# Three expert routers of a one-core transformer kernel without their unread TensorE products

## The chip, the cores and the metric

The kernel runs on one NeuronCore of a Trainium2 chip. The metric is the device time of one execution in microseconds. Five engines work side by side and meet at semaphores: TensorE (PE: matmuls; PEld: its weight loads), VectorE (DVE), ScalarE (ACT), GpSimd (POOL) and SyncE (SP), which issues the weight transfers.

## The reference

A sequence of 256 tokens of width 1024 goes through three layers, all in float32. Each has a mixer and a mixture of experts:

```python
x = x + token_mixer(rms_norm(x), ...)              # first block
x = x + hierarchical_moe(rms_norm(x), ...)         # 32 experts, hidden width 256   ("one")
x = layer_norm(ALPHA * x + even_mixer(x), ...)     # second block, layer 0
x = layer_norm(ALPHA * x + hierarchical_moe_2(x))  # 32 experts, hidden width 512   ("l0")
x = layer_norm(ALPHA * x + fourier_mixer(x), ...)  # second block, layer 1
x = layer_norm(ALPHA * x + hierarchical_moe_2(x))  # 32 experts, hidden width 512   ("l1")
```

A router takes, for each token, the best of four groups of eight experts, then the two best experts of that group, and weighs them by a softmax. An expert computes `(silu(x @ w_gate) * (x @ w_up)) @ w_down` on the tokens that chose it. The weights of all experts are read: 101 MB for stage one (32 x 3 x 1 MB) and 201 MB each for l0 and l1 (32 x 3 x 2 MB).

## The kernel before, in words

For each of the three expert layers, tagged one, l0 and l1, the kernel runs `stage_out_route` and then `stage_experts`, which calls `stage_packed`.

`stage_out_route` is the end of the mixer and the router, on two halves of 128 tokens (j = 0, 1). TensorE multiplies the mixer's result by the output weights (`out`, L1713, four groups), turns the normalised rows with transposes (`turn`, L1721) and computes 36 logits a token (`logits`, L1729). VectorE adds the residual and normalises a half (L1828 in one, L1831 and L1832 in l0 and l1) before TensorE may turn it; ScalarE copies the turned rows into `hT` (L1767) before the logits may read them. When both halves' logits are there, VectorE reads them (L1862 with a bias, L1864 without) and selects groups and experts in a chain of small operations, ending at `sel` (L1877). TensorE then counts, with ten small matmuls (L1750), how many tokens an expert has and the place of each; VectorE reads the places at L1898 (l0, l1) or L1908 (one).

`keep_busy(k, bank, n)` (L199) issues n matmuls of the identity with itself, 128 x 512, into a PSUM bank that nobody reads; each is two matmul instructions in the profile (L203). In the router they stand at three places of TensorE's queue: after the first half's logits, after the second half's logits, and after the counts. There are 4, 3 and 2 in stage one, 4, 3 and 1 in l0, and 4, 2 and 1 in l1. TensorE takes its queue in order and does not wait for anything before one of them.

`stage_packed` gathers the tokens of a pass by multiplication with one-hot tiles, which VectorE makes first (L2299). The first gather (L2147, L2148) is 32 matmuls of 128 columns, ScalarE copies it into `hT` (L2263), and a pass follows: gate product, up product, down product (L2154), with SiLU on ScalarE (L2271). Stage one has eleven passes of three experts, the other two have sixteen passes of two. In stage one alone a single `keep_busy` stands ahead of the first gather (L2207).

Weights come in chunks through a ring in on-chip memory: seven chunks of 3 MB in stage one, eleven of 2 MB in l0 and l1. SyncE issues the transfer of a chunk (L2034 in one, L2036 in l0 and l1) when `s_used` says that the chunk whose place it takes has been multiplied. Before the router has ended the ring is filled ahead; the next transfer then waits for the first chunk that the gate product of pass 0 releases. The same queue also carries the next stage's small tables and weights.

Of the kernel before, what the change touches and what calls it, by code (L numbers as in the profile page):

```python
# [192 lines left out]
def bc(ap, axis, n):  # L193

    shape = list(ap.shape)
    return ap.unsqueeze(axis).broadcast_to(shape[:axis] + [n] + shape[axis:])


def keep_busy(k, bank, n):  # L199

    ident = k.table("ident")
    for _ in range(n):
        k.nc.tensor.matmul(bank, ident, bc(ident, 1, W // P), start=True, stop=True)  # L203
# [1382 lines left out]
class FinalTail:  # L1586

    tag = "final"
# [64 lines left out]
def stage_out_route(k, tag, alpha, rr, ex, ahead, rows_first=None):  # L1653
# [15 lines left out]
    with scope:  # L1669
# [21 lines left out]
        tp = k.ps(f"turned_ps_{tag}", [P, 2, W])  # L1691
# [8 lines left out]
        with nc.Block() as block:  # L1700
            @block.sync
            def _(sp):
                ahead(sp, s_y)
                if bias is None:
                    sp.wait_ge(s_t, 4)
                    sp.wait_ge(s_low, NJ)
                    ex.load(sp, 1)

            @block.tensor
            def _(pe):  # L1710
                def out(j, n):
                    for c in range(KC):
                        last = nc.tensor.matmul(y[:, j, n, :], k.hT[:, c, j * P:(j + 1) * P],  # L1713
                                                w_out[:, c, n * W:(n + 1) * W], start=(c == 0), stop=(c == KC - 1))
                    last.then_inc(s_y, 1)

                def turn(j):
                    pe.wait_ge(s_h, j + 1)
                    for n in range(2):
                        for c in range(4):  # L1720
                            last = nc.tensor.transpose(turned[2 * j + n][:, c * P:(c + 1) * P],  # L1721
                                                       rows[:, j, 4 * n + c:D:KC], k.table("ident"))
                        last.then_inc(s_t, 1)

                def logits(j):
                    for c in range(KC):
                        if c % 4 == 0:
                            pe.wait_ge(s_ht, 2 * j + c // 4 + 1)
                        last = nc.tensor.matmul(lp[:, j, :], k.hT[:, c, j * P:(j + 1) * P], w[:, c, :],  # L1729
                                                start=(c == 0), stop=(c == KC - 1))  # L1730
                    last.then_inc(s_p, 1)

                pe.wait_ge(k.s_out_w, k.out_loads)
                out(0, 0)
                out(0, 1)
                out(1, 0)
                turn(0)
                out(1, 1)
                pe.wait_ge(s_wl, 16)
                logits(0)  # L1740
                keep_busy(k, tp[:, 0], 4)
                turn(1)
                logits(1)
                keep_busy(k, tp[:, 0], 2 if tag == "l1" else 3)
                pe.wait_ge(s_sel, 1)
                pe.wait_ge(s_rl, 16 if w_bias is None else 32)
                for j in (NJ, *range(NJ)):
                    for i in range(min(j + 1, NJ)):
                        t = before if i == j else ones
                        last = nc.tensor.matmul(counts if j == NJ else pp[:, j], t, sel[:, i], start=(i == 0),  # L1750
                                                stop=(i == min(j, NJ - 1)))
                    if j >= NJ - 1:
                        last.then_inc(s_pos, 1)
                keep_busy(k, tp[:, 0], 2 if ex.ways == 3 else 1)

            @block.scalar
            def _(act):
# [762 lines left out]
class EvenTail:  # L2520

    tag = "f"
# [477 lines left out]
class FourierTail:  # L3000

    tag = "fourier"
# [333 lines left out]
```

## Time and profile before

| what | value |
|---|---|
| median of 3 runs | 1812.33 us (1811.42 to 1812.88) |
| the profiled execution's own time | 1813.08 us |
| its span, first to last instruction | 1809.5 us |
| mean granted TensorE clock | 0.981 |
| TensorE busy | 93% of the span |
| VectorE, ScalarE, GpSimd busy | 37%, 22%, 3% |
| read from memory | 578.62 MB |

A timeline row has the start in microseconds from the span's start, the duration, the engine, the line of the kernel, the operation, what it writes and reads, its shape, and in brackets how long the engine had been idle before it and what it waited for. Rows of one line that follow each other are merged, with their count (x8). Durations of matmuls include their latency, so that pipelined ones overlap: the pitch is read from starts. The granted clock (PEclk) is a share of 2.4 GHz: 1.00 is 2.4 GHz, 0.50 is 1.2 GHz.

### The profile page before, as it was taken

The page shows a single profiled execution, that of the slowest core. Times are in us where ns is not written, and L with a number is a line of the kernel's source. Part 1 is how long each engine was busy: PE and PEld are TensorE (multiplying, and loading weights), DVE is VectorE, ACT ScalarE, POOL GpSimd, SP SyncE. Part 2 cuts the span into 40 slices and gives each one's busy share as a digit, 9 for nine tenths or more (in the row PEclk, how much of TensorE's full clock was granted, in tenths as well). Part 3 has the DMA queues.
Part 4 walks back from the last instruction along what each step waited for, and adds up shares of the span by engine and source line. Part 5 has one row for each costly group of instructions (what it writes and reads, how often), then busy time and mean ns, then how long its engine had stood idle before and what let it go on. Part 6 is the DMA issues. An engine that isn't in the chain of part 4 may idle for free. (4 is left out here: it accounts for less than half of the span.)

```text
span 1809.5 us, 21999 instructions
## 1 busy us (share of the span) xinstructions
PE 1678.2 (93%) x9162; PEld 875.4 (48%) x9162; DVE 661.0 (37%) x1392; ACT 389.8 (22%) x690; POOL 62.6 (3%) x67
## 2 busy tenths in 40 slices
PE   7999999999998779999999999889979999999895
PEld 6785445684654445555344444334543444434442
DVE  3468576563442235443222212122441122222123
ACT  2411333342222122312111111011211111111111
POOL 0000000600000003100000000000000000000000
PEclk9999999999999999999999999999989999999998
DMA  5343432109899978448999999999958999999995
GB/s 216 137 132 140 160 119 51 48 23 427 339 429 428 429 329 311 158 179 359 423 428 428 427 427 428 427 428 419 420 231 370 428 427 427 428 428 426 427 424 207
DMA packets 66949, 583.28 MB, mean 322 GB/s; under 512 B 19420, under 2 KB 21596, under 8 KB 31774
## 3 DMA queue, kind: packets, MB, share of 16 engines
q1 hardware_dynamic: 62093, 580.21, 77.6%
q10 hardware_dynamic: 4752, 1.61, 0.5%
q8 instruction: 75, 1.23, 0.3%
q14 instruction: 29, 0.23, 0.0%
HBM read 578.62 MB, written 3.15 MB: 321 GB/s over the span
## 5 line engine op out<-in xcount | busy, mean ns | idle before, releaser
L2154 PE MATMUL up_ps_l<-room,hT 128*64 128x512 f32 x800 | 214.3, 600 | 10.9 <-DMA room<-in_expert_w_up 9.4
L2154 PE MATMUL gate_ps_l<-room,hT 128*64 128x512 f32 x704 | 197.2, 601 | 13.3 <-DMA room<-in_expert_w_gate 7.8
L2154 PE MATMUL y_ps_l<-room,hidden_l 128*64 128x512 f32 x736 | 202.0, 595 | 4.3 <-ACT hidden_l L2278 2.3
L415 PE MATMUL proj_ps<-room,hT 128*128 128x512 f32 x288 | 124.6, 592 | 0.0
L2154 PEld LDWEIGHTS up_ps_l<-room,hT 128*64 128x64 f32 x800 | 67.9, 138 | 114.3 <-issue 113.5
L2154 PEld LDWEIGHTS gate_ps_l<-room,hT 128*64 128x64 f32 x704 | 63.9, 138 | 117.7 <-issue 117.7
L2377 DVE SCALAR_TENSOR_TENSOR y_low_l<-y_ps_l,slot_gate_l,y_high_l 128x512 fp32r<-128x512 f32 x64 | 47.9, 751 | 193.8 <-ACT y_high_l L2288 193.8
L2154 PE MATMUL gate_ps_l<-late_room,hT 128*64 128x512 f32 x320 | 113.6, 616 | 1.5 <-DMA late_room<-in_expert_w_gate 1.4
L2154 PEld LDWEIGHTS y_ps_l<-room,hidden_l 128*64 128x64 f32 x736 | 63.6, 137 | 105.4 <-issue 95.0
L407 PE MATMUL proj_ps<-hT,room 128*128 128x256 f32 x512 | 113.6, 384 | 0.0
L407 PEld LDWEIGHTS proj_ps<-hT,room 128*128 128x128 f32 x512 | 98.1, 192 | 15.3 <-issue 1.8
L2154 PE MATMUL y_ps_l<-late_room,hidden_l 128*64 128x512 f32 x288 | 102.8, 596 | 1.5 <-ACT hidden_l L2278 1.2
L2367 DVE TENSOR_TENSOR hidden_l<-hidden_l,up_ps_l 128x512 f32<-128x512 f32 x32 | 22.0, 687 | 214.6 <-PE up_ps_l L2154 214.6
L2288 ACT ACTIVATE y_high_l<-y_ps_l,slot_gate_l 128x512 fp32r<-128x512 f32 x64 | 44.0, 687 | 205.7 <-PE y_ps_l L2154 205.3
L2154 PE MATMUL up_ps_l<-late_room,hT 128*64 128x512 f32 x224 | 84.9, 595 | 2.8 <-DMA room<-in_expert_w_up 1.4
L415 PEld LDWEIGHTS proj_ps<-room,hT 128*128 128x128 f32 x288 | 54.7, 190 | 66.7 <-issue 66.5
L2271 ACT ACTIVATE hidden_l<-gate_ps_l 128x512 f32<-128x512 f32 x32 | 34.7, 1086 | 217.6 <-PE turn_ps_l L2221 217.6
L2314 DVE SCALAR_TENSOR_TENSOR x<-x,gather_ps_l 128x512 f32<-128x512 f32 x64 | 42.5, 684 | 97.7 <-PE gather_ps_l L2182 97.6
L2147 PE MATMUL gather_ps_l<-onehot_l,h_high_l 128*128 128x256 f32 (+1 forms) x288 | 73.5, 293 | 2.0 <-DVE onehot_l L2299 2.0
L2263 ACT ACTIVATE hT<-gather_ps_l 128x512 f32<-128x512 f32 x64 | 38.2, 597 | 169.0 <-PE gather_ps_l L2148 169.0
L2148 PE MATMUL gather_ps_l<-onehot_l,h_low_l 128*128 128x256 f32 (+1 forms) x288 | 72.1, 288 | 0.0
L2147 PEld LDWEIGHTS gather_ps_l<-onehot_l,h_high_l 128*128 128x128 f32 x288 | 57.1, 198 | 6.1 <-DVE onehot_l L2299 3.9
(636 smaller groups left out, 2347.5 us busy)
## 6 DMA issues: line engine op xcount, KB each, us to landing
room<-in_expert_w_up SPq DMA_DIRECT2D x50, 2048.0 KB, 28.2
room<-in_expert_w_down SPq DMA_DIRECT2D x46, 2048.0 KB, 33.2
room<-in_expert_w_gate SPq DMA_DIRECT2D x44, 2048.0 KB, 31.2
room<-in_moe_by_pass SPq DMA_DIRECT2D x22, 3072.0 KB, 30.5
late_room<-in_expert_w_gate SPq DMA_DIRECT2D x20, 2048.0 KB, 28.8
late_room<-in_expert_w_down SPq DMA_DIRECT2D x18, 2048.0 KB, 24.4
room<-in_w_in_blocks SPq DMA_DIRECT2D x17, 2048.0 KB, 8.0
late_room<-in_expert_w_up SPq DMA_DIRECT2D x14, 2048.0 KB, 32.0
```

The lines of the kernel that those rows point to most:

```text
L407: last = mm(pp[:, n % 2, m * T:(m + 1) * T], wbuf[n % 2][:, c, m * P:(m + 1) * P], k.hT[:, c, :], start=(c == 0), stop=(c == KC - 1))
L415: last = mm(pp[:, n % 2, j * W:(j + 1) * W], k.hT[:, c, j * P:(j + 1) * P], wbuf[n % 2][:, c, :], start=(c == 0), stop=(c == KC - 1))
L2147: mm(at, k.h_high[:, j, c], moving, start=(j == 0), stop=False)
L2148: last = mm(at, k.h_low[:, j, c], moving, start=False, stop=(j == NJ - 1))
L2154: return mm(of[q * TW:(q + 1) * TW], lhsT, rhs, **flags)
L2263: nc.scalar.activation(xg(n * per[b], per[b])[:, :, 0:width], got, ACT.Copy).then_inc(s_xg, 1)
L2271: nc.scalar.activation(hid[:].rearrange("p (c n) -> p n c", c=HT), G[:, 0:H].rearrange("p (n c) -> p n c", c=HT), ACT.Silu).then_inc(s_sg, 1)
L2288: nc.scalar.activation(yh[:, n], Y[:, n], ACT.Copy, scale=slot_gate[:, 0:1]).then_inc(s_yh, 1)
L2314: nc.vector.scalar_tensor_tensor(out=xs, in0=xs, scalar=1.0 if p else alpha, in1=scatter_bank[o], op0=ALU.mult, op1=ALU.add).then_inc(s_ad ...
L2367: nc.vector.tensor_tensor(hidden, hidden, Up[:, 0:H].rearrange("p (n c) -> p c n", c=HT), ALU.mult).then_inc(s_hid, 1)
L2377: nc.vector.scalar_tensor_tensor(out=yl[:, n], in0=Y[:, n], scalar=slot_gate[:, 0:1], in1=yh[:, n].bitcast(F32), op0=ALU.mult, op1=ALU.sub ...
```

## The change

The three calls of `keep_busy` in `stage_out_route` are taken out, for all three stages. The single call in `stage_packed` (L2207) and those of other stages stay.

```diff
                 logits(0)
-                keep_busy(k, tp[:, 0], 4)
                 turn(1)
                 logits(1)
-                keep_busy(k, tp[:, 0], 2 if tag == "l1" else 3)
                 pe.wait_ge(s_sel, 1)
                 pe.wait_ge(s_rl, 16 if w_bias is None else 32)
                 for j in (NJ, *range(NJ)):
...
                     if j >= NJ - 1:
                         last.then_inc(s_pos, 1)
-                keep_busy(k, tp[:, 0], 2 if ex.ways == 3 else 1)
```

## Rows read from the trace of the kernel before

**Rows 1.** Timeline of stage l0, from its second turn to the first transfer:

```profile
826.48 1.16 PE L1721 MATMUL out_ps_l<-tables,x 128*128 128x128 f32 x8 [0.64 <-DVE x L1832]
...
827.88 1.97 PE L1729 MATMUL logit_ps_l<-router_w_l,hT 128*128 128x36 f32 x16 [0.24 <-ACT hT L1767]
...
829.99 0.23 DVE L1862 TENSOR_TENSOR logits_l<-logit_ps_l,router_b_l 128x72 f32<-128x72 f32 x1 [0.33 <-PE logit_ps_l L1729]
...
833.51 0.83 PE L1750 MATMUL place_ps_l<-sel_l,router_tables_l 128*128 128x32 f32 x6
...
834.63 0.22 DVE L1898 SCALAR_TENSOR_TENSOR place<-place_ps_l,sel_l 128x64 f32<-128x64 f32 x1
...
835.74 0.43 DVE L2299 TENSOR_TENSOR onehot_l<-tables,place 128x256 fp32r<-128x256 f32 x1 [0.43 <-PEq L1700]
...
836.23 0.33 PE L2147 MATMUL gather_ps_l<-onehot_l,h_high_l 128*128 128x128 f32 x1 [0.94 <-DVE onehot_l L2299]
...
839.94 5.37 PE L2154 MATMUL gate_ps_l<-late_room,hT 128*64 128x512 f32 x24
...
843.64 0.33 SPq L2036 DMA_DIRECT2D late_room<-in_expert_w_down  x1
```

**Rows 2.** Timeline of stage l1, from its first turn to the first transfer:

```profile
1322.55 1.97 PE L1721 MATMUL turned_ps_l<-tables,x 128*128 128x128 f32 x8 [6.29 <-DVE x L1832]
...
1323.70 0.60 ACT L1767 ACTIVATE hT<-turned_ps_l 128x512 f32<-128x512 f32 x1 [11.91 <-PE turned_ps_l L1721]
...
1345.11 0.83 PE L1750 MATMUL place_ps_l<-sel_l,router_tables_l 128*128 128x32 f32 x6
...
1346.58 0.22 DVE L1898 SCALAR_TENSOR_TENSOR place<-place_ps_l,sel_l 128x64 f32<-128x64 f32 x1
...
1347.69 0.42 DVE L2299 TENSOR_TENSOR onehot_l<-tables,place 128x256 fp32r<-128x256 f32 x1 [0.43 <-PEq L1700]
...
1348.17 0.47 PE L2147 MATMUL gather_ps_l<-onehot_l,h_high_l 128*128 128x128 f32 x1 [1.08 <-DVE onehot_l L2299]
...
1355.19 6.13 PE L2154 MATMUL gate_ps_l<-late_room,hT 128*64 128x512 f32 x16
...
1361.36 0.33 SPq L2036 DMA_DIRECT2D late_room<-in_expert_w_down  x1
```

**Rows 3.** Timeline of stage one, second half to the first transfer:

```profile
455.19 1.28 DVE L1828 SCALAR_TENSOR_TENSOR late_room<-x,rstd_one,gain_one 128x1024 f32<-128x1024 f32 x1
...
457.15 1.05 PE L1721 MATMUL out_ps_one<-tables,late_room 128*128 128x128 f32 x8
...
460.55 0.23 DVE L1864 COPY logits_one<-logit_ps_one 128x72 f32<-128x72 f32 x1
...
464.07 0.83 PE L1750 MATMUL place_ps_one<-sel_one,router_tables_one 128*128 128x33 f32 x6
...
466.31 0.23 DVE L1908 SCALAR_TENSOR_TENSOR taken_one<-place_ps_one,sel_one 128x66 f32<-128x66 f32 x1
...
468.15 1.10 PE L203 MATMUL scatter_ps_one<-tables 128*128 128x512 f32 x2 [1.45 <-PEq L1700]
...
476.42 0.33 SPq L2034 DMA_DIRECT2D room<-in_moe_by_pass  x1
```

**Rows 4.** Timeline of ScalarE, SiLU of the last pass of l0 and l1:

```profile
1253.62 1.08 ACT L2271 ACTIVATE hidden_l<-gate_ps_l 128x512 f32<-128x512 f32 x1 [6.57 <-PE turn_ps_l L2221]
...
1771.16 1.08 ACT L2271 ACTIVATE hidden_l<-gate_ps_l 128x512 f32<-128x512 f32 x1 [6.57 <-PE turn_ps_l L2221]
```

**Rows 5.** The page's throughput, 40 equal slices of 45.2 us each:

```profile
GB/s 216 137 132 140 160 119 51 48 23 427 339 429 428 429 329 311 158 179 359 423 428 428 427 427 428 427 428 419 420 231 370 428 427 427 428 428 426 427 424 207
```

**Rows 6.** Windows: engines' busy time, then PEclk, DMA share, GB/s (last three):

```profile
838.00:840.00 2.00, 2.00 (x21) 1.93 (x20) 0.00 (x0) 0.60 (x1) 0.00 (x0) 1.00 0.08 33
1345.00:1347.00 2.00, 2.00 (x11) 1.06 (x10) 1.24 (x7) 0.14 (x1) 0.00 (x0) 0.89 0.02 4
1359.00:1361.00 2.00, 2.00 (x8) 0.52 (x6) 0.00 (x0) 0.00 (x0) 0.00 (x0) 0.70 0.00 0
```

## Prediction

> **What bounds the kernel now.** I first asked which wait decides the end of an expert stage. In the timeline of both layer stages, l0 and l1, SyncE's first weight transfer after the router is issued when the first product group of pass 0 frees its chunk: at 843.64 us in l0 [rows 1] and at 1361.36 us in l1 [rows 2]. The reader should set beside these the SiLU of the last pass, at 1253.62 and 1771.16 us [rows 4]: 409.98 and 409.80 us later. The two stages reached that first transfer very differently, and from there on they are the same length to 0.2 us. The page's throughput row says why: 419 to 428 GB/s in every slice but the routers' and the turns between layers [rows 5]. So from its first transfer on a stage runs at the pace of the weights, and a microsecond by which that transfer comes later is a microsecond at the end. Until it comes, the ring is full and the queue stands still: 33 GB/s at 838 to 840 us and 0 at 1359 to 1361 us [rows 6]. The router, the first gather and the first gate product therefore lie on the path that sets the end.
>
> Next I asked how l0 and l1 differ there. From the one-hot (L2299) to that transfer, l0 takes 843.64 - 835.74 = 7.90 us and l1 takes 1361.36 - 1347.69 = 13.67 us: 5.77 us more for the same work. The windows show the granted clock at 1.00 in l0's gather; in l1 it falls to a mean of 0.89 at 1345 to 1347 us and is still only 0.70 on average at 1359 to 1361 us [rows 6], that is, it stood at 1.2 of 2.4 GHz between. What TensorE had done before is the point: l1's middle group of unread products is one product shorter than l0's, and nothing else in the router's code differs on TensorE. A second place tells the same: in l1 the first turn began after 6.29 us of idle, and its eight transposes then took 1.97 us [rows 2] where l0's second turn took 1.16 us [rows 1].
>
> **The change part by part.** All 24 products of `keep_busy` in the three routers go: nine in one, eight in l0, seven in l1, two matmul instructions each. They are read by nobody and no other engine waits for them; only TensorE's own queue stands behind them. What they hold up today is small: in stage one the rows of half 1 are ready at 455.19 + 1.28 = 456.47 us, but the turn's first transpose starts at 457.15 us, behind the unread products [rows 3]. In l0 the turn starts after 0.64 us of idle [rows 1], so there nothing is won. No DMA is moved and no wait is added.
>
> What takes their place is idle time. Between the first logits and the second turn TensorE has nothing to do, nor between the second logits and the selection, nor from there to the one-hot; in these 14 us of l0 (822 to 836) only transposes, 36-column logits and 32-column counts are left. l1 shows that less of a loss of work than this brings the clock to half, so I take it that it falls in all three routers, before the second turn or during it, and stays at half through the gather, as in l1. There is no row of a router without any of the products; the bounds are no fall at all (nothing below) and half speed from the second turn to the first transfer.
>
> Step 1, second turn and logits. At full clock, turn start to logits end is 827.88 + 1.97 - 826.48 = 3.37 us in l0, and VectorE waits for it (0.33 us of idle before L1862) [rows 1]. At half clock the first copy of the turned rows ends 1323.70 + 0.60 - 1322.55 = 1.75 us after the turn starts [rows 2]. The pitch at half clock comes from the gather: its 32 matmuls take 1355.19 - 1348.17 = 7.02 us in l1, 0.22 us each [rows 2], against 839.94 - 836.23 = 3.71 us, 0.116 us each, in l0 [rows 1], where a logit matmul takes 1.97 / 16 = 0.123 us. So sixteen logits need 3.5 us, and the end is 5.3 us after the turn: 1.9 us late in l0 and, with the same instructions, in l1. In stage one the turn starts earlier, at 456.5, and ends its logits at 461.8; VectorE took them at 460.55 without having waited [rows 3]: 1.3 us late. Bounds: 0 to 2.
>
> Step 2, counts and places, ten matmuls of the same pitch: 1.0 us longer at half clock. Cover: in l0 they end at 833.51 + 0.83 = 834.34 and are read at 834.63, so 0.7 us comes through [rows 1]; in l1 they end at 1345.94 and are read at 1346.58: 0.35 us [rows 2]; in one, 464.90 against 466.31: hidden [rows 3]. The products behind them go; they ended before VectorE's last operation in each stage, so nothing is won.
>
> Step 3, the one product that stays, at the start of stage one's experts (1.10 us for two instructions at L203 [rows 3]), runs at half clock: 0.4 to 1.1 us, I take 0.85 (one pitch of some 0.43 us for each of the two).
>
> Step 4, the first gather at half clock: 7.02 - 3.71 = 3.3 us in one and in l0. Stage l1 pays this today.
>
> Step 5, the gate product up to the first chunk's release: 843.64 - 839.94 = 3.70 us at full clock [rows 1], 1361.36 - 1355.19 = 6.17 us in l1, where the clock came back on the way [rows 2, 6]. Where it comes back will differ from execution to execution, so the loss is between 0 and 3.7 us; l1's 2.5 is one draw. I take 1.7, near the middle, for one and l0, and also for l1, which then gains 0.8 on the profiled execution.
>
> Sum: one 1.3 + 0.85 + 3.3 + 1.7 = 7.15; l0 1.9 + 0.7 + 3.3 + 1.7 = 7.6; l1 1.9 + 0.35 - 0.8 = 1.45; together 16.2 us. The profiled execution's own time is 1813.08 (span 1809.5 and 3.6 around it), 0.75 above the median of the runs: 1813.1 + 16.2 = **1829.3 us**. What is late next: each stage's weight queue, by its stage's sum; the even stage and the Fourier tail move with it unchanged, since they wait for the same queue and for TensorE.
>
> That idle time lowers the clock is also what the Trainium skill says, in "TensorE: Matmul & The Clock Gate" (section "Terms"); its price is the throttled time times the share of pulses lost, there one half. By that, l1's stretch would have cost about 6.8 us, where the difference to l0 is 5.77. Its sum is the second rival.
>
> **The rivals.**
> (a) The clock comes back sooner, in the middle of the gather. Against it: in l1 the whole gather ran at the slow pitch [rows 2]. Then step 4 costs 1.7 and step 5 nothing: one 1.3 + 0.85 + 1.7 = 3.85, l0 4.3, l1 2.25 + 1.7 - 5.8 = -1.85; sum 6.3, time 1819.4.
> (b) Everything between fall and return costs half its length, waits included. l1's stretch now begins at about 1346.56 us (0.89 on average over 2 us is 0.44 us at half), 1.1 us before its one-hot, and ends at about 1360.2 (0.70 is 1.2 us at half) [rows 6]: some 13.7 us; it would begin about 9.3 us before the one-hot (826.48 to 835.74 in l0 [rows 1]) and hold the 2 to 3 us of steps 1 and 2: some 25 us in each stage. Halves: 12.5 + 12.5 + (12.5 - 6.8) = 30.7, time 1844. Against it: VectorE's chain of small operations sets most of the router and has no part in TensorE's clock.
> (c) No change: what remains is enough to hold the clock, or the ring covers the delay. For it: the clock held through l0's idle of 0.94 us before the gather [rows 1]. Against it: l1's difference, and 410 us after the first transfer in both stages. Time 1812 to 1813.
> (d) Faster: the clock falls in l1 because of the unread product that runs last there, not for want of work; without it l1's gather would run as l0's, 5.8 us sooner: 1807.3. It decides if the windows show 1.00 through l1's gather. Against it: l0 runs the same last product and keeps its clock [rows 6].
>
> **How the numbers follow.** Forecast 0.78, (a) 0.09, (b) 0.05, (c) 0.05, (d) 0.03. The forecast's own range: at the low end step 5 costs nothing, stage one's clock falls only during the turn (0.7) and its product costs 0.4: 4.4 + 5.9 - 0.25 = 10, 1823; at the high end step 5 costs 3.7 everywhere, step 2 is uncovered and step 3 costs 1.1: 9.4 + 9.9 + 4.1 = 23.4, 1836.5. With (a) taken in: 1820 to 1837. A measurement of this kernel tells 0.2%, some 3.6 us, from no change; the forecast, (a) and (b) are slower by more: 0.92; same 0.05, faster 0.03.
>
> **What would show it.** Granted clock 0.50 from the second turn on in all three stages, and through the first gather; gather matmuls 0.21 us apart; first transfers some 7 us later after the router's start in one and l0 and 1 to 2 us in l1; 410 us from there to the last SiLU, as now. A clock of 1.00 in l0's gather would prove me wrong; so would a last SiLU less than 409 us after a late first transfer, since then the delay was absorbed. If the clock stays at half into the next products, (b) is nearer.

## The result and the profile after

The changed kernel takes 1824.17 us (median of 7 executions, 1818.49 to 1829.89) beside 1812.45 us for the kernel before (7 executions, 1810.12 to 1816.97): 11.7 us more, ratio 1.0063, 95% interval 1.0049 to 1.0078. The forecast was 1829.3 in a range of 1820 to 1837, so the direction and the range held and the size was too large. The profiled execution is the fastest of the seven: span 1816.8 us, time 1818.49.

First the timeline of the changed kernel's stage l0, as [rows 1]; lines of the kernel are two or three lower than before, where products went.

```profile
824.63 1.97 PE L1721 MATMUL out_ps_l<-tables,x 128*128 128x128 f32 x8 [4.15 <-DVE x L1829]
...
830.20 0.23 DVE L1859 TENSOR_TENSOR logits_l<-logit_ps_l,router_b_l 128x72 f32<-128x72 f32 x1 [2.37 <-PE logit_ps_l L1729]
...
834.14 1.47 PE L1748 MATMUL place_ps_l<-sel_l,router_tables_l 128*128 128x32 f32 x6
...
835.75 0.23 DVE L1895 SCALAR_TENSOR_TENSOR place<-place_ps_l,sel_l 128x64 f32<-128x64 f32 x1 [0.93 <-PE place_ps_l L1748]
...
836.86 0.43 DVE L2296 TENSOR_TENSOR onehot_l<-tables,place 128x256 fp32r<-128x256 f32 x1 [0.43 <-PEq L1700]
...
837.34 0.47 PE L2144 MATMUL gather_ps_l<-onehot_l,h_high_l 128*128 128x128 f32 x1 [1.74 <-DVE onehot_l L2296]
...
844.36 6.06 PE L2151 MATMUL gate_ps_l<-late_room,hT 128*64 128x512 f32 x22
...
849.17 0.33 SPq L2033 DMA_DIRECT2D late_room<-in_expert_w_down  x1
```

VectorE's wait for the logits has grown from 0.33 to 2.37 us, a wait of 0.93 us for the places is new, and the gather's first matmul to the gate product takes 7.02 us where it took 3.71. The same for l1, as [rows 2]:

```profile
1343.18 1.97 PE L1721 MATMUL out_ps_l<-tables,x 128*128 128x128 f32 x8 [4.16 <-DVE x L1829]
...
1348.75 0.23 DVE L1859 TENSOR_TENSOR logits_l<-logit_ps_l,router_b_l 128x72 f32<-128x72 f32 x1 [2.37 <-PE logit_ps_l L1729]
...
1355.40 0.43 DVE L2296 TENSOR_TENSOR onehot_l<-tables,place 128x256 fp32r<-128x256 f32 x1 [0.43 <-PEq L1700]
...
1362.90 4.91 PE L2151 MATMUL gate_ps_l<-late_room,hT 128*64 128x512 f32 x16
...
1367.86 0.33 SPq L2033 DMA_DIRECT2D late_room<-in_expert_w_down  x1
```

Here the one-hot to the gate product is 7.50 us, as before the change, and the gate product to the transfer 4.96 instead of 6.17. Stage one, as [rows 3], goes another way:

```profile
446.35 1.87 PE L1729 MATMUL logit_ps_one<-router_w_one,hT 128*128 128x36 f32 x16
...
449.62 1.28 DVE L1825 SCALAR_TENSOR_TENSOR late_room<-x,rstd_one,gain_one 128x1024 f32<-128x1024 f32 x1
...
450.96 1.97 PE L1721 MATMUL out_ps_one<-tables,late_room 128*128 128x128 f32 x8 [2.73 <-DVE late_room L1825]
...
456.52 0.23 DVE L1861 COPY logits_one<-logit_ps_one 128x72 f32<-128x72 f32 x1 [1.60 <-PE logit_ps_one L1729]
...
464.12 0.42 DVE L2296 TENSOR_TENSOR onehot_one<-tables,room 128x256 fp32r<-128x256 f32 x1 [0.77 <-PEq L1700]
464.13 2.04 PE L203 MATMUL scatter_ps_one<-tables 128*128 128x512 f32 x2 [2.21 <-PEq L1700]
...
467.36 0.41 PE L2145 MATMUL gather_ps_one<-onehot_one,h_low_one 128*128 128x128 f32 x1
...
468.00 0.28 PE L2145 MATMUL gather_ps_one<-onehot_one,h_low_one 128*128 128x128 f32 x1
...
470.44 3.66 PE L2151 MATMUL gate_ps_one<-room,hT 128*32 x64
...
474.16 0.33 SPq L2031 DMA_DIRECT2D room<-in_moe_by_pass  x1
```

The gather's matmuls fall from 0.41 to 0.28 us in the middle of it, and the gate product runs at full speed. The windows of the changed kernel say the same in the granted clock (third from the right), as [rows 6]:

```profile
466.00:468.00 2.00, 2.00 (x12) 2.00 (x11) 1.17 (x5) 0.00 (x0) 0.00 (x0) 0.56 0.00 0
468.00:470.00 2.00, 2.00 (x20) 2.00 (x20) 0.00 (x0) 0.60 (x1) 0.00 (x0) 1.00 0.00 0
838.00:840.00 2.00, 2.00 (x12) 2.00 (x11) 0.40 (x1) 0.00 (x0) 0.00 (x0) 0.50 0.00 0
845.00:847.00 2.00, 2.00 (x8) 0.61 (x6) 0.00 (x0) 0.06 (x1) 0.00 (x0) 0.59 0.00 0
1357.00:1359.00 2.00, 2.00 (x11) 2.00 (x11) 0.30 (x1) 0.00 (x0) 0.00 (x0) 0.50 0.00 0
1364.00:1366.00 2.00, 2.00 (x10) 0.49 (x8) 0.00 (x0) 0.00 (x0) 0.00 (x0) 0.63 0.00 0
```

In l0 and l1 TensorE has 1.2 of 2.4 GHz through the whole gather and gets the rest back in the gate product; in stage one it got it back near the end of the window 466 to 468, in the gather. The last SiLU of l0 and of l1 (ScalarE's timeline, as [rows 4]) come 410.26 and 410.03 us after the first transfers, and the page's throughput outside the routers is as in [rows 5]:

```profile
1259.43 1.09 ACT L2268 ACTIVATE hidden_l<-gate_ps_l 128x512 f32<-128x512 f32 x1 [6.57 <-PE turn_ps_l L2218]
...
1777.89 1.09 ACT L2268 ACTIVATE hidden_l<-gate_ps_l 128x512 f32<-128x512 f32 x1 [6.57 <-PE turn_ps_l L2218]
```

```profile
GB/s 215 140 163 147 142 93 51 48 89 428 309 428 429 428 285 368 98 243 270 425 427 428 427 428 427 428 427 419 419 234 358 427 428 427 427 428 427 427 424 205
```

So in l0 and l1 nothing absorbed the delay. The measure that follows all runs is the stretch from the start of the first half's logits (L1729) to the first transfer behind the gather. In l0 it begins at this row, before and after:

```profile
820.46 1.87 PE L1729 MATMUL logit_ps_l<-router_w_l,hT 128*128 128x36 f32 x16
```

```profile
818.61 1.87 PE L1729 MATMUL logit_ps_l<-router_w_l,hT 128*128 128x36 f32 x16
```

The stretches before are 24.49, 23.18 and 29.30 us in one, l0 and l1; after 27.81, 30.56 and 30.71, that is +3.32, +7.38 and +1.41, together 12.1 us. The profiled spans differ by only 7.3 because this execution reached its first router at 446.35 us and the one before at 451.93: a difference of 5.6 us that lies ahead of all that was changed. From the first router's start to the end of the span the changed kernel took 1370.4 us where the kernel before took 1357.6: 12.8 us more.

A part of the timed difference lies outside the span. Wherever the record has both, the device time is 3.2 to 4.6 us longer than the span in the executions of the kernel before, and 1.6 to 2.8 us longer in those of every other kernel here, even of one that differs from it by a single product. No run shows why. So each timed difference to the kernel before is some 1.8 us lower than the difference of the spans, and the clock has no part in that: the median span is 1822.5 us in the changed kernel and 1809.5 to 1810.2 in the kernel before, 12 to 13 us apart.

### The profile page after: what moved, and what is told of

Its sections match the earlier page's. It is cut to its first block and busy times, and to the rows that moved or that the text cites. A ratio compares the mean times of both kernels' runs of the same rounds, so it can differ in the third digit from the quotient of the medians.

```text
span 1816.8 us, 21903 instructions
## 1 busy us (share of the span) xinstructions
PE 1670.1 (92%) x9114; PEld 878.7 (48%) x9114; DVE 661.8 (36%) x1392; ACT 390.1 (21%) x690; POOL 62.9 (3%) x67
## 3 DMA queue, kind: packets, MB, share of 16 engines
q8 instruction: 74, 1.21, 0.3%
```

## The experiments

The theory: idle time in the router brings the clock to 1.2 GHz, and what this costs until the first transfer is the loss. Each expectation names its rival; the first is a fixed price for each product, whatever the clock does. "Before" in this section is the median of the executions of the kernel before on the same chip: 1813.69 us for the first four runs, 1814.26 for the second four, 1813.17 for the last four. A gain or loss in per cent is that of the ratio on record, which is not the ratio of the two medians: for the first run they are 2.8 us apart and the ratio gives 3.8, for the second 4.4 and 6.0. The table has the stretches of all profiled executions and, without the part outside the span, the median span less that of the kernel before, which the scatter of the executions leaves open by 2 or 3 us (an estimate from the spans on record). All are in microseconds:

| kernel | one | l0 | l1 | ratio of times, 95% interval | median span |
|---|---|---|---|---|---|
| before | 24.49 | 23.18 | 29.30 | |  |
| before, again | 24.50 | 23.18 | 29.41 | 0.9993 (0.9979 to 1.0008) | -0.90 |
| changed | 27.81 | 30.56 | 30.71 | 1.0063 (1.0049 to 1.0078) | +12.3 to +13.0 |
| changed, again | 32.49 | 30.48 | 30.69 | 1.0065 (1.0043 to 1.0087) | +15.55 |
| without one's products | 32.56 | 26.49 | 27.88 | 1.0021 (1.0009 to 1.0033) | +4.95 |
| without l0's | 24.50 | 30.70 | 29.36 | 1.0033 (1.0018 to 1.0047) | +6.50 |
| without l1's | 24.50 | 23.19 | 30.66 | 0.9995 (0.9982 to 1.0007) | +1.40 |
| l1 with three | 24.50 | 23.18 | 26.80 | 0.9989 (0.9975 to 1.0002) | +0.10 |
| without the first group | 25.65 | 29.09 | 30.52 | 1.0009 (0.9992 to 1.0027) | +4.45 |
| without the two others | 30.06 | 29.35 | 29.91 | 1.0043 (1.0027 to 1.0059) | +9.05 |
| changed, one product ahead | 31.37 | 32.63 | 33.14 | 1.0091 (1.0073 to 1.0108) | +18.55 |
| changed, none ahead | 30.35 | 31.82 | 30.93 | 1.0071 (1.0051 to 1.0091) | +15.15 |
| four behind the logits | 24.50 | 26.49 | 26.83 | 0.9974 (0.9959 to 0.9989) | -3.35 |
| more products | 24.49 | 23.53 | 23.89 | 0.9960 (0.9946 to 0.9975) | -6.05 |

**One stage at a time.** The three calls are skipped for one tag, here one (the first call is shown); the other two runs do the same for l0 and l1.

```diff
-                keep_busy(k, tp[:, 0], 4)
+                if tag != "one":
+                    keep_busy(k, tp[:, 0], 4)
...
```

> The nine unread products go in stage one's router alone. Theory (idle time halves the granted clock, and the delay of the first weight transfer is the cost): from the first half's logits to stage one's first transfer 27.8 us, as in the changed kernel, where the kernel before has 24.5; l0 and l1 as before; time +3.3 us (+0.2%). Rival (each product that goes costs the same, by whatever it displaces in the queue: 11.7 us for 24 products, 0.49 each): +4.4 us.

> The eight unread products go in l0's router alone. Theory: granted clock 0.50 from before the second turn to inside the first gate product, first transfer some 30.5 us after the first half's logits instead of 23.2; time +7.4 us (+0.4%), the greatest of the three stages. Rival (0.49 us for each product): +3.9 us, less than for stage one.

> The seven unread products go in l1's router alone. Theory: the gather runs at half clock in the kernel before too, so only the second turn, the logits and the counts get longer: first transfer 30.7 us after the first half's logits instead of 29.3; time +1.4 us, within 0.2%. Rival (0.49 us for each product): +3.4 us.

Measured: 1816.50 us (+0.21%, 3.8 us), 1818.05 us (+0.33%, 6.0 us) and 1812.92 us (-0.05%, not to be told from none; in the spans +1.40 us, and the stretch 30.66, both as expected). Each stage's loss lies in its own router. The intervals do not tell l0's loss from one's, but l1's seven products cost less than the 3.4 us of a fixed price. But stage one's stretch was 32.56 us here and not 27.81. The timeline and then a window of this kernel's stage one:

```profile
469.88 2.04 PE L203 MATMUL scatter_ps_one<-tables 128*128 128x512 f32 x2 [2.21 <-PEq L1700]
...
478.57 6.03 PE L2157 MATMUL gate_ps_one<-room,hT 128*32 x64
...
484.67 0.33 SPq L2037 DMA_DIRECT2D room<-in_moe_by_pass  x1
```

```profile
478.00:480.00 2.00, 2.00 (x20) 1.19 (x23) 0.00 (x0) 1.30 (x2) 0.00 (x0) 0.50 0.00 0
```

The clock was still at half when the gate product began, which took 6.03 us instead of 3.66. And l0, whose code was that of the kernel before, lost 3.3 us in this execution (26.49 instead of 23.18); the clock of l0's gather:

```profile
844.00:846.00 2.00, 2.00 (x17) 2.00 (x16) 0.00 (x0) 0.60 (x1) 0.00 (x0) 0.81 0.23 98
846.00:848.00 2.00, 2.00 (x11) 1.83 (x12) 0.00 (x0) 0.23 (x1) 0.00 (x0) 0.50 0.00 0
```

So l0's code keeps the clock in one execution and not in another. [Rows 1] is a draw, one outcome of several, and I had taken it for what the code of the stage does. In l1 the clock fell in all four profiles of the code of [rows 2]; there only the return differed, with stretches from 27.88 to 29.41 us.

**l1 with the same number as l0.**

```diff
-                keep_busy(k, tp[:, 0], 2 if tag == "l1" else 3)
+                keep_busy(k, tp[:, 0], 3)
```

> The kernel before with three unread products instead of two after l1's second logits, as l0 has. Theory: the granted clock stays at 1.00 through l1's gather, which takes 3.7 instead of 7.0 us, and the first transfer comes some 5 to 6 us earlier after the router's start: 23.2 to 24 us after the first half's logits; time -5.5 us (-0.3%). Rival (the clock falls in l1 because of the unread products that run last, or has no price): no gain, 0 to +0.5 us.

Measured: 1811.47 us, ratio 0.9989 with an interval that holds 1. The expected 5.5 us did not come, and the time is the one that the rival gave (no gain). l1's timeline and one window of this kernel:

```profile
1351.12 0.33 PE L2147 MATMUL gather_ps_l<-onehot_l,h_high_l 128*128 128x128 f32 x1 [1.29 <-DVE onehot_l L2299]
...
1356.69 5.06 PE L2154 MATMUL gate_ps_l<-late_room,hT 128*64 128x512 f32 x16
...
1361.80 0.33 SPq L2036 DMA_DIRECT2D late_room<-in_expert_w_down  x1
```

```profile
1354.00:1356.00 2.00, 2.00 (x11) 2.00 (x11) 0.00 (x0) 0.00 (x0) 0.00 (x0) 0.50 0.04 8
```

The gather began at full clock (0.33 us for its first matmul, 0.47 in [rows 2]) and lost it on the way. With one product more the fall came later in this execution; the idle time between the counts and the gather was left. My reading of l1, that one product made its difference to l0, falls with this in its simple form.

**Which group.** Only the first group (12 of 24 products), or only the two others (the other 12, not 15 as the expectation says), are taken out.

```diff
                 logits(0)
-                keep_busy(k, tp[:, 0], 4)
                 turn(1)
```

```diff
                 logits(1)
-                keep_busy(k, tp[:, 0], 2 if tag == "l1" else 3)
...
-                keep_busy(k, tp[:, 0], 2 if ex.ways == 3 else 1)
```

> Only the first group goes (four products in each router, ahead of the second turn); the groups behind the second logits and behind the counts stay. Theory (idle time halves the granted clock, the delay of the first weight transfer is the cost): the clock falls before the second turn, turn to logits' reading takes 5.6 instead of 3.5 us, the middle group runs at half clock and so ends after the selection, read to one-hot 1 to 3 us longer; the products bring the clock back by the gather, which takes 4.2 to 4.6 us from the one-hot in most stages. One and l0 +3 to +5 us each, l1 +1 to +4; together +5 to +13. Rival (only the work next to the gather matters): 0 to +2 us.

> The first group stays, the two behind the second logits and behind the counts go (15 ... of 24 products: five in one, four in l0, three in l1, with the first group's twelve kept). Theory: the second turn and the logits stay at full speed (3.4 to 3.5 us); the clock falls between the logits and the one-hot, so the gather takes 6.3 to 8.7 us from the one-hot in one and 7.5 in l0 and l1, the gate product 3.7 to 6.2: +2 to +8 in one, +4.5 to +6.5 in l0, 0 in l1; time +5 to +12 us. Rival (the loss lies in the turn and logits): 0 to +2 us.

Without the first group: 1816.79 us, ratio 1.0009, not to be told from none, as the rival gave; in the spans +4.45 us, just under the expected 5 to 13. The middle group of l0 before the change, then l0's timeline and windows in this run:

```profile
829.68 2.82 PE L203 MATMUL turned_ps_l<-tables 128*128 128x512 f32 x6
```

```profile
834.50 4.32 PE L203 MATMUL turned_ps_l<-tables 128*128 128x512 f32 x6
...
852.32 0.33 SPq L2035 DMA_DIRECT2D late_room<-in_expert_w_down  x1
```

```profile
838.00:840.00 2.00, 2.00 (x13) 1.50 (x12) 1.02 (x7) 0.39 (x2) 0.00 (x0) 1.00 0.50 201
846.00:848.00 2.00, 2.00 (x7) 0.65 (x9) 0.00 (x0) 0.60 (x1) 0.00 (x0) 0.50 0.00 0
```

The middle group's three products, begun at half clock (4.32 us for six instructions, where 2.82 is their time at full clock), were still running when the clock came back, and it stood at 1.00 before the gather; in this execution it had fallen once more by the gate product. Without the two other groups: 1821.40 us, ratio 1.0043. Turn and logits stayed at full speed (3.51 us in l0), the clock fell behind them, and the gather was slow:

```profile
848.50 7.77 PE L2152 MATMUL gate_ps_l<-late_room,hT 128*64 128x512 f32 x26
...
854.16 0.33 SPq L2034 DMA_DIRECT2D late_room<-in_expert_w_down  x1
```

From the one-hot at 841.00 to the gate product it is 7.50 us again. By ratio and by span the two groups behind the second logits are worth more than the first: 0.43% and 9.05 us beside 0.09% and 4.45.

**The product at the head of the experts.** It is put into all three stages of the changed kernel, or taken out of stage one.

```diff
-                if ex.ways == 3:
-                    keep_busy(k, SC[:], 1)
+                keep_busy(k, SC[:], 1)
```

```diff
-                if ex.ways == 3:
-                    keep_busy(k, SC[:], 1)
```

> The changed kernel with the one product that stays at the head of stage one's experts put at the head of l0's and l1's too. Theory: it costs 0.9 to 1.8 us at half clock ahead of the gather but can bring the clock back inside the gather, as in stage one of the changed kernel (one-hot to gate 6.3, gate 3.7 us) or not (8.7 and 6.1, as in another execution of stage one); against the changed kernel 0 to -4 us. Rival (the clock's return has nothing to do with it): +1.8 to +3 us against the changed kernel.

> The changed kernel without the one product at the head of stage one's experts. Theory: at half clock this product costs what the gather waits for it, 8.70 - 7.50 = 1.2 us; one-hot to gate 7.2 to 7.5 us and gate product 4.8 to 6.2 in stage one, as in l0 and l1; against the changed kernel -1 us where the clock does not come back early in that, +1 to +4 where it does. Rival (it keeps the clock up): +4 us.

Measured: 1830.59 us (ratio 1.0091) with it in all three, 1826.65 us (1.0071) without any. The first is about 5 us slower than the changed kernel's 1.0063 and 1.0065, with intervals that overlap, so the expected gain did not come and the rival's loss did, greater than its 1.8 to 3 us; l0's timeline with it:

```profile
845.45 2.04 PE L203 MATMUL scatter_ps_l<-tables 128*128 128x512 f32 x2 [1.25 <-PEq L1700]
...
854.14 7.35 PE L2151 MATMUL gate_ps_l<-late_room,hT 128*64 128x512 f32 x24
```

One-hot to gate product is 8.69 us beside 7.50 without it: on a half clock already fallen, one product costs 1.2 us in front of the gather and did not bring the clock back in the gather of any of the three stages (8.69, 8.70 and 8.70 us). Without any, stage one shows the expected 7.50 us and a gate product of 5.06, its stretch 2.1 us shorter than in the second profile of the changed kernel; the times are not to be told apart, and the rival's 4 us did not come.

**Both kernels once more.**

> The kernel before once more, for a second profile. Theory (the clock's fall differs between executions even where the code is the same): ratio 1.000; in l0 or l1 the stretch from the first half's logits to the first transfer may differ from the first profile's 23.2 and 29.3 us, anywhere between 23.2 and 29.5, and it is longer exactly where the granted clock is at 0.50. Rival (the clock's course is fixed by the code): 24.5, 23.2 and 29.3 us again, to 0.2.

> The changed kernel once more, for a second profile and more timed executions. Theory: ratio to before 1.006 to 1.009; l0 and l1 take 30 to 32 us from the first half's logits to the first transfer, as in the first profile; stage one takes 30 to 32.6 us, if the early return of the clock in the first profile (27.8 us) was one draw. Rival (the product that stays brings the clock back in stage one): 27.8 us again.

The kernel before: 1812.36 us, ratio 0.9993, its three stretches within 0.11 us of the first profile's. That is what the rival gave; two profiles of this kernel show no difference between its executions. That executions differ rests on l0 in the run without one's products, and on the changed kernel: 1827.03 us, ratio 1.0065, and stage one at 32.49 us:

```profile
481.39 5.94 PE L2151 MATMUL gate_ps_one<-room,hT 128*32 x64
...
487.40 0.33 SPq L2031 DMA_DIRECT2D room<-in_moe_by_pass  x1
```

The early return of the first profile was a draw. This profile's three stretches exceed those of the first profile before by 8.00, 7.30 and 1.39 us, 16.7 in all; from the first router's start to the end it is 15.2 us.

**More products.** If idle time is the cause, filling the rest of it should gain. Four products behind the second logits in all stages, with or without one at the head of the experts in all stages:

```diff
-                keep_busy(k, tp[:, 0], 2 if tag == "l1" else 3)
+                keep_busy(k, tp[:, 0], 4)
...
-                if ex.ways == 3:
-                    keep_busy(k, SC[:], 1)
+                keep_busy(k, SC[:], 1)
```

> The kernel before with four products behind the second logits in all three stages and one product at the head of the experts in all three. Theory: the clock stays at 1.00 through all three routers and first gathers in nearly every execution: 24.5 us from the first half's logits to the first transfer in one, 23.5 in l0, 23.5 to 24 in l1 (29.3 before in the profiled execution); time -3 to -6 us against the kernel before, and a narrower spread. Rival (products cost their time, 0.43 to 0.86 us each, and bring nothing back): +0.5 to +2 us.

> The kernel before with four products behind the second logits in all three stages, but none at the head of l0's and l1's experts: one part of the faster version alone. Theory: between the counts and the gather TensorE has one product in some 2 us, so in part of the executions the clock still falls there: 23.2 us in l0 and l1 where it holds, 26 to 29 where it falls; time between the kernel before and the faster version, -2 to -6 us. Rival (the middle group alone decides): -7.3 us, as the faster version.

Measured: 1806.11 us (1802.05 to 1807.34, 7 executions), ratio 0.9960, which is 7.3 us of 1814.26 faster than the kernel before; in the spans it is 6.05 us, in the three stretches 5.05. With the middle group alone it is 1808.31 us, ratio 0.9974, 3.35 us in the spans. The intervals of the two do not tell them apart; in its profile the clock still fell in both layers' gathers (26.49 and 26.83 us), and the three stretches are no shorter than before (77.82 us beside 76.97), so this one profile does not show where that gain lies. The timeline of l1 in the faster version, and windows behind the logits and in the gather:

```profile
1347.53 1.10 PE L203 MATMUL scatter_ps_l<-tables 128*128 128x512 f32 x2 [0.76 <-PEq L1700]
...
1352.08 3.65 PE L2154 MATMUL gate_ps_l<-late_room,hT 128*64 128x512 f32 x16
...
1355.77 0.33 SPq L2036 DMA_DIRECT2D late_room<-in_expert_w_down  x1
```

```profile
1344.00:1346.00 2.00, 2.00 (x13) 1.47 (x12) 1.22 (x10) 0.44 (x2) 0.00 (x0) 1.00 0.00 0
1350.00:1352.00 2.00, 2.00 (x20) 2.00 (x18) 0.00 (x0) 0.60 (x1) 0.00 (x0) 1.00 0.00 0
```

The clock is 1.00 in both windows, l1's stretch is 23.89 us, and the closing product of the router, which rival (d) blamed, is still there.

## Why the prediction held, and where it was too large

**The bound.** That the first transfer sets the end held in l0 and l1 in every profile: 409.4 to 410.9 us from it to the last SiLU. Rival (c) falls by this; l0's full 7.4 us are in the end. For stage one the prediction showed no such row, and there it holds only in part: from its first transfer to l0's first logits it is 344.0 to 344.7 us in the nine profiles with a stretch of up to 27.8 us, and 342.1 to 342.8 in the five with a stretch of 30 or more. So 1.2 to 2.6 us of a long delay in stage one are made up before l0; no run shows where.

**Step 1**, turn and logits: forecast 1.9, 1.9 and 1.3 us for l0, l1 and one. Turn start to the reading of the logits went from 3.51 to 5.57 us in l0 (+2.06), and l1 shows the same 5.57; in one, ready rows to reading went from 4.08 to 5.62 (+1.54). Right, 0.2 us short each.

**Step 2**, counts and places: forecast 0.7, 0.35 and 0; the reading to the one-hot grew by 0.91, 0.55 and 0. Right.

**Steps 3 and 4**, one-hot to gate product: l0 from 4.20 to 7.50, +3.30 as forecast. In one 4.15 were forecast; the first profile had 6.32 - 4.55 = 1.77, the second 8.69 - 4.55 = 4.14.

**Step 5**, gate product: forecast 1.7 in one and l0, -0.8 in l1; measured 1.11 in l0 and -1.21 in l1, in one 0 in the first profile and 2.29 in the second.

The sum of 16.2 us was therefore near what the second profile's stretches show (16.7), and too large for the timed executions, 11.7 us (ratios 1.0063 and 1.0065). Three terms were mis-sized. The 3.6 us around the span were carried over from the kernel before; in the changed kernel they are 1.6 to 2.5, so some 1.8 us of the miss lie outside all that the sum is about. Stage one, forecast at 7.15, costs 3.8 us (0.21%) alone and 4.95 in the spans: its gather and gate product, 3.3 + 1.7, are paid only where the clock does not come back in the gather (steps 3 to 5 together, forecast at 5.85, were 1.77 us in the first profile and 6.43 in the second), and where they are paid, a part is made up before l0. And l0, forecast at 7.6, costs 6.0 us (0.33%) alone and 6.50 in the spans; before the change it is not always at full clock, 26.49 us in one of five profiles with its code, which accounts for a part of this. For stage one's gather and for l0 before the change I had read one course of the clock as the stage's fixed one. How often the clock falls or comes back in each case is not settled by these profiles. In the spans the single stages add up to 12.85 us, beside 12 to 13 and 15.55 for all three in the changed kernel; in the ratios they add up to 0.49% beside 0.63%, since the part outside the span enters each of them.

**The rivals.** (a), a return inside the gather, happened in one of the five profiles of stage one without its router's products, and in none of the five each of l0 and l1. (b), half of every microsecond at half clock, is out: l0's stretch at half clock, from before the second turn at 824.63 us to within the window 845 to 847, is at least 20 us, its half 10, and the stage lost 7.38. The price by throttled time in the Trainium skill, "TensorE: Matmul & The Clock Gate" (section "Terms"), goes with that rival and is too high here, because VectorE's chain fills much of the stretch: from the reading of the logits to the one-hot l0 lost only 0.91 of 6.66 us. (d) is refuted by the change itself, since l1 takes 7.50 us from the one-hot to the gate product without its closing product too, and by the faster version, which keeps that product and has the gather at full clock. No run separates idle time from the small matmuls of the router as the reason for the fall.

## What to carry to other kernels

Products that nobody reads can be worth keeping: look at what follows them, and price the stretch at half clock from the last event that starts the bounding stream (here the first weight transfer), not from TensorE's busy share. Here the groups nearer to the TensorE-bound stretch were worth more than the one further ahead, and a gap left between them and it could undo them. Where the clock's course differs between executions, take the profile of one execution as a draw, look at the same code in the profiles of the other runs, and range the forecast over both. Compare the spans as well as the times: a part of a timed difference can lie outside the span.

## What the runs showed of the hardware that was not expected

At half clock the first gather's 32 matmuls, issued one behind the other for 7.02 us at a pitch of 0.22, did not bring the clock back in l0 or l1, while it came back during three unread products ahead of the gather (1.00 at 838 to 840 us without the first group). The granted clock of the same code differed between executions: l0 held it in four of five profiles and lost it in one, and stage one of the changed kernel got it back in the gather in one profile and not in the next. And one unread product costs 0.35 us ahead of the gather at full clock (4.55 us from one-hot to gate product in l0 of the faster version, 4.20 before), 1.2 us at half.
